# A 64-row tile with high and low halves in one stationary operand, and attention tails by Newton steps on GpSimd

## The reference, cut to what matters

```python
h = rmsnorm(x, norm_x)                      # x: 1024 prompt rows, 64 sample rows, 1024 wide
aq, ak, av, az, gq, gk, gv, gz, gr, mq, mz, gl = split(h @ w_in)
aq, ak = rmsnorm(aq per 64, g_qa), rmsnorm(ak per 64, g_ka)
p = softmax(aq @ ak.T / 8 + alibi, causal)  # two maps a head; samples also attend to paged keys
oa = (p[0] - lam * p[1]) @ av
oa = rmsnorm(oa per 128, g_oa) * (1 - lam_init)
ua = (oa * silu(az)) @ w_branch[0]
ub = (rmsnorm(gla(gq, gk, gv, gr), g_ob) * silu(gz)) @ w_branch[1]
um = (softmax(rmsnorm(mq per 128, g_qm) @ mem_k.T) @ mem_v * silu(mz)) @ w_branch[2]
y = x + (sigmoid(g_a) * ua + sigmoid(g_b) * ub + sigmoid(g_m) * um) @ w_o
```

## Time and profile before

| | |
|---|---|
| Median of three runs | 1357.0 us (1356.37 to 1358.52) |
| The profiled execution | 1358.5 us, of which the span 1356.7 us |
| PE | busy 1292.0 us, 95% of the span, 7846 matmuls |
| DVE | 546.9 us, 40% |
| ACT | 477.3 us, 35% |
| GpSimd | 108.5 us, 8% |
| PE's clock | nine tenths of full speed or more in 37 of the page's 40 slices, eight tenths in three |

### The profile page before, as it was taken

The page is one execution under the profiler, slowest core; times in us unless marked ns, Lnnn a source line. Parts: engine busy times, 40 slices in busy tenths (PEclk is TensorE's granted clock), DMA queues, the critical chain, the costliest instruction groups (busy, mean ns, idle before and its releaser), DMA issues.

```text
span 1356.7 us, 19404 instructions
## 1 busy us (share of the span) xinstructions
PE 1292.0 (95%) x7846; PEld 1115.6 (82%) x7846; DVE 546.9 (40%) x1187; ACT 477.3 (35%) x1064; POOL 108.5 (8%) x126
## 2 busy tenths in 40 slices
PE   6999999999877899999899999999999999999998
PEld 5778788888756786788777887788999999999876
DVE  5654344566673325277743443312222222222411
ACT  5543223655665225256632433212221111212200
POOL 0010000000001000000111000000122221222000
PEclk9999999999998899999899999999999999999999
DMA  8432111110004331101212303431011131110422
GB/s 273 145 101 82 47 39 44 32 32 20 13 0 153 92 114 33 32 24 45 80 49 69 103 24 105 129 113 47 24 47 48 47 109 47 47 48 17 155 86 70
DMA packets 89930, 94.47 MB, mean 70 GB/s; under 512 B 8498, under 2 KB 64626, under 8 KB 89714
## 3 DMA queue, kind: packets, MB, share of 16 engines
q1 hardware_dynamic: 85506, 79.33, 19.3%
q0 software_dynamic: 4336, 13.90, 2.8%
HBM read 79.32 MB, written 13.89 MB: 69 GB/s over the span
## 4 chain that ended last, share of the span: by engine, by line
PE 87%; ACT 5%; DVE 4%; issue 2%; DMA 1%; SPq 0%; POOLq 0%; POOL 0%; ACTq 0%; DVEq 0%
PE heavy L835 14%; PE heavy L837 14%; PE heavy L836 14%; PE heavy L847 9%; PE heavy L849 8%; PE heavy L848 8%; PE heavy L897 4%; PE scores L947 2%; PE attended L967 1%; PE transposed L956 1%; PE scores L1208 1%; PE transposed L924 1%; PE scores L1107 1%; PE attended L1226 1%; ACT arena L1496 1%
## 5 line engine op out<-in xcount | busy, mean ns | idle before, releaser
L1369 ACT ACTIVATE arena<-heavy 128x364 f32<-128x364 f32 (+1 forms) x108 | 50.9, 471 | 366.4 <-PE heavy L837 366.3
L835 PE MATMUL heavy<-h_hi,rc_hi 128*128 128x364 f32 (+1 forms) x384 | 131.9, 343 | 0.0
L836 PE MATMUL heavy<-h_lo,rc_hi 128*128 128x364 f32 (+1 forms) x384 | 127.4, 332 | 0.0
L837 PE MATMUL heavy<-h_hi,rc_lo 128*128 128x364 f32 (+1 forms) x384 | 127.4, 332 | 0.0
L835 PE MATMUL heavy<-h_hi,rp_hi 128*128 128x364 f32 (+1 forms) x384 | 126.3, 329 | 0.0
L836 PE MATMUL heavy<-h_lo,rp_hi 128*128 128x364 f32 (+1 forms) x384 | 126.1, 328 | 0.0
L837 PE MATMUL heavy<-h_hi,rp_lo 128*128 128x364 f32 (+1 forms) x384 | 126.1, 328 | 0.0
L1824 DVE SCALAR_TENSOR_TENSOR arena<-arena,heavy 128x364 f32<-128x364 f32 (+1 forms) x48 | 25.5, 532 | 211.4 <-PE heavy L837 211.4
L614 POOL TENSOR_TENSOR merged<-merged,arena 128x364 f32<-128x364 f32 (+1 forms) x48 | 66.8, 1392 | 441.7 <-DVE arena L1824 441.7
L835 PEld LDWEIGHTS heavy<-h_hi,rc_hi 128*128 128x128 f32 x384 | 73.7, 192 | 4.0 <-issue 3.1
L836 PEld LDWEIGHTS heavy<-h_lo,rc_hi 128*128 128x128 f32 x384 | 73.6, 192 | 0.0
(11 more groups left out here) (312 smaller groups left out, 2896.5 us busy)
## 6 DMA issues: line engine op xcount, KB each, us to landing
out<-arena POOLq DMA_DIRECT2D x36, 256.0 KB, 3.3
rc_whole<-w_in SPq DMA_DIRECT2D x16, 512.0 KB, 3.9
rp_whole<-w_in SPq DMA_DIRECT2D x16, 512.0 KB, 4.0
arena<-x_prompt SPq DMA_DIRECT2D x8, 512.0 KB, 5.7
arena<-cache_k_a SPq DMA_DIRECT2D x16, 256.0 KB, 3.2
arena<-cache_v_a SPq DMA_DIRECT2D x16, 256.0 KB, 3.5
ra_whole<-w_in SPq DMA_DIRECT2D x8, 512.0 KB, 4.1
arena<-cache_mem_k SPq DMA_DIRECT2D x8, 512.0 KB, 4.6
```

Of the source, the lines that this page charges most:

```text
L835: nc.tensor.matmul(out, a_hi, b_hi, start=(x == 0), stop=False)
L836: nc.tensor.matmul(out, a_hi, b_lo, start=False, stop=False)
L837: end = nc.tensor.matmul(out, a_lo, b_hi, start=False, stop=(x == len(terms) - 1))
L1369: nc.scalar.activation(tanh[m % 2][:, 0:cw], bank[:, 0:cw], ACT.Tanh, scale=0.5)\
```

## The change

Two things are changed. **The sample tile's products.** `h_hi` is widened by 64 columns, so that for the sample tile the high half and the low half stand side by side as one stationary operand of 128 (`sample_product`). Two matmuls a slice, by the weights' high and low half, make 16 instead of 24; rows 0 to 63 of the bank then hold the products of the high half, rows 64 to 127 those of the low half. ACT copies the lower 64 rows to SBUF, DVE adds them onto the upper ones, and from there on the work is as before. DVE makes the low half a second time, into the widened columns. In V the sample tile now stands before tile 7, in Q behind tile 0, and in the second half of O before tile 7.

**The tails of the prompt.** ACT takes the squares only; no other table is loaded. One unit later DVE adds the epsilon term and makes a first guess of the reciprocal root by integer arithmetic (`tail_guess`); GpSimd improves it by three Newton steps of four instructions on 128x4 elements, each waiting for the one before (`tail_newton`); DVE scales without a reciprocal. The tails of the other branches and of the samples are as before.

For room, one table (`comb`, 64 KB) is moved into the shared arena, and its transfer stands behind the first value pages in SP's queue; PE's first `sample_weights` waits for it. The core of the diff:

```diff
-    add("V", [("rows", "gv", r) for r in range(PT + 1)])
+    add("V", [("rows", "gv", r) for r in (*range(PT - 1), PT, PT - 1)])
     add("MZ", cols("mz", KW))
-    add("Q", [("rows", "mq", r) for r in range(PT + 1)])
+    add("Q", [("rows", "mq", r) for r in (0, PT, *range(1, PT))])
     add("PA", pairs(0))
     add("PB", pairs(1))
     add("PM", pairs(2))
-    add("O", [("out", r, j) for j in range(2) for r in range(PT + 1)])
+    add("O", [("out", r, 0) for r in range(PT + 1)] + [("out", r, 1) for r in (*range(PT - 1), PT, PT - 1)])
...
-        h_hi, h_lo, h_whole = trio("h", 0, 8704, [KD, T])
+        h_hi = part("h_hi", -TAIL, [KD, T + NS_TOK])
+        h_lo, h_whole = part("h_lo", 8704, [KD, T]), part("h_whole", 8704, [KD, T], F32)
...
+            def settle(ins):
+                steps[0] += 1
+                ins.then_inc(newton, 1)
+                pool.wait_ge(newton, steps[0])
+            def tail_newton(k):
+                x, y, a = ostat[:, 0, :], ostat[:, 2, :], ohalf[:, :]
+                pool.wait_ge(guessed, k + 1)
+                for i in range(3):
+                    settle(pool.tensor_tensor(out=a, in0=y, in1=y, op=ALU.mult))
+                    settle(pool.tensor_tensor(out=a, in0=a, in1=x, op=ALU.mult))
+                    settle(pool.tensor_scalar(a, a, -0.5, 1.5, ALU.mult, ALU.add))
+                    end = pool.tensor_tensor(out=y, in0=y, in1=a, op=ALU.mult)
+                    if i < 2:
+                        settle(end)
+                end.then_inc(oroot_done, 1)
+            for k in range(PT - 1):
+                tail_newton(k)
...
+            tail_newton(PT - 1)
...
+            sp.wait_ge(pv_done, NU)
+            sp.dma_start(comb, tab["comb"]).then_inc(comb_in, 16)
...
+            def sample_product(n, kind, bank):
+                w_hi, w_lo, _ = W4[kind]
+                for k in range(KD):
+                    both = h_hi[:, k, NP_TOK:T + NS_TOK]
+                    nc.tensor.matmul(bank[:, :], both, w_hi[:, k, :], start=(k == 0), stop=False)
+                    end = nc.tensor.matmul(bank[:, :], both, w_lo[:, k, :], start=False, stop=(k == KD - 1))
+                end.then_inc(hv_full[n % 2], 1)
...
+                    if t == PT:
+                        sample_product(n, kind, bank)
+                        return
...
+                if b == 0:
+                    pe.wait_ge(comb_in, 16)
...
+                    if sample_rows(n):
+                        nc.scalar.copy(low_rows_of(n), bank[NS_TOK:P, :]).then_inc(low_rows, 1)
+                        act.wait_ge(rows_added, sample_rows(n))
...
-                    settle(nc.scalar.activation(waste[:, :], og[:, h * P:(h + 1) * P], ACT.Square,
-                                                accum_out=ostat[:, 0, h:h + 1]))
-                for h in range(H):
-                    end = nc.scalar.activation(ostat[:, 1, h:h + 1], ostat[:, 0, h:h + 1], ACT.Sqrt,
-                                               bias=ssq[:, h:h + 1], scale=1.0 / P)
-                end.then_inc(oroot_done, 1)
+                    end = nc.scalar.activation(waste[:, :], og[:, h * P:(h + 1) * P], ACT.Square,
+                                               accum_out=ostat[:, 0, h:h + 1])
+                    if h < H - 1:
+                        settle(end)
+                end.then_inc(squares_done, 1)
+                act.wait_ge(squares_done, k + 1)
...
+                if sample_rows(n):
+                    dve.wait_ge(low_rows, sample_rows(n))
+                    nc.vector.tensor_tensor(out=bank[0:NS_TOK, :], in0=bank[0:NS_TOK, :], in1=low_rows_of(n), op=ALU.add)\
+                        .then_inc(rows_added, 1)
...
+                if t == PT:
+                    hi, _, whole = tile_of(t)
+                    low((hi, sample_low, whole))
...
+            def tail_guess(k):
+                x, y = ostat[:, 0, :], ostat[:, 2, :]
+                dve.wait_ge(squares_done, k + 1)
+                settle(nc.vector.scalar_tensor_tensor(out=x, in0=x, scalar=1.0 / P, in1=ssq[:, :], op0=ALU.mult, op1=ALU.add))
+                settle(nc.vector.tensor_scalar(y.bitcast(I32), x.bitcast(I32), 1, None, ALU.logical_shift_right))
+                nc.vector.tensor_scalar(y.bitcast(I32), y.bitcast(I32), -1, 0x5F3759DF, ALU.mult, ALU.add).then_inc(guessed, 1)
             def tail_scale(k):
                 n = tail_rows(k)
                 dve.wait_ge(oroot_done, k + 1)
-                settle(nc.vector.reciprocal(ostat[0:n, 2, :], ostat[0:n, 1, :]))
+                if k >= PT:
+                    settle(nc.vector.reciprocal(ostat[0:n, 2, :], ostat[0:n, 1, :]))
...
+                if u - 1 in A_END:
+                    tail_guess(A_END[u - 1])
...
+            tail_guess(PT - 1)
             tail_scale(PT - 1)
```

More of the change, by code:

```diff
@@ L87, in shape_tables @@
     return {k: np.ascontiguousarray(v, dtype=np.float32) for k, v in tabs.items()}
-SMALL = ["ident", "batch", "slope", "isl", "map", "comb", "gmask"]
+SMALL = ["ident", "batch", "slope", "isl", "map", "gmask"]
 def heavy_jobs():
@@ L264, in hybrid_step @@
         arena_base = -(-nc.sbuf_base // 32) * 32
-        arena = sb("arena", [P, 51928])
+        TAIL = 512
+        arena = sb("arena", [P, TAIL + 51928])
         def shaped(v, shape):
@@ L311, in hybrid_step @@
         vpage = [at(41472 + 1024 * i, [NPG, W]) for i in range(2)]
+        comb = at(44544, [P])
         past_t, new_t = at(43520, [PAST]), at(43776, [NB, NS_TOK])
@@ L370, in hybrid_step @@
         gx, gmem = sb("gx", [P, KD]), sb("gmem", [P, KD])
-        gka_row, gkm_row = sb("gka_row", [P, 64]), sb("gkm_row", [P, P])
+        gka_row, gkm_row = at(51712, [64]), at(21504, [P])
         ba_col = sb("ba_col", [P, 2])
@@ L376, in hybrid_step @@
         rstat = sb("rstat", [P, 3])
-        ostat = sb("ostat", [P, 3, H])
+        ostat, ohalf = sb("ostat", [P, 3, H]), sb("ohalf", [P, H])
         ssum, ssq, waste = sb("ssum", [P, 2, H]), sb("ssq", [P, H]), sb("waste", [P, P])
@@ L413, in hybrid_step @@
         qpad_zero, qpad_ready, new_keys = sem("qpad_zero"), sem("qpad_ready"), sem("new_keys")
-        tabs_in, pt_in = sem("tabs_in"), sem("pt_in")
+        tabs_in, comb_in, pt_in = sem("tabs_in"), sem("comb_in"), sem("pt_in")
         k_in, v_in = [sem("k_in0"), sem("k_in1")], [sem("v_in0"), sem("v_in1")]
@@ L418, in hybrid_step @@
         o_full, o_free, oroot_done = sem("o_full"), sem("o_free"), sem("oroot_done")
+        guessed, squares_done, newton = sem("guessed"), sem("squares_done"), sem("newton")
         ob_free = sem("ob_free")
@@ L436, in hybrid_step @@
         lam_exp = sem("lam_exp")
+        low_rows, rows_added = sem("low_rows"), sem("rows_added")
         def map_of(u, c):
@@ L445, in hv_wait_free, with sample_rows, low_rows_of @@
             eng.wait_ge(hv_free[n % 2], n // 2 + 1)
+        def sample_rows(n):
+            j = JOBS[n]
+            if (j[0], j[1]) == ("out", PT) or (j[0] == "rows" and j[2] == PT):
+                return sum(1 for x in JOBS[:n + 1] if (x[0], x[1]) == ("out", PT) or (x[0] == "rows" and x[2] == PT))
+            return 0
+        sample_low = h_hi[:, :, T:T + NS_TOK]
+        def low_rows_of(n):
+            kind = "out" if JOBS[n][0] == "out" else JOBS[n][1]
+            return {"gv": at(TL, [W]), "mq": sq_m, "out": at(44544, [W])}.get(kind, sq)[0:NS_TOK, :]
         def bc(ap, k):
@@ L557, in _ @@
                         pool.dma_start(mk_kept, mk_first).then_inc(mk_out, 16)
+            steps = [0]
+            def settle(ins):
[15 more added lines that the diff above has]
+                tail_newton(k)
             pool.wait_ge(sc_read, 2 * NU)
@@ L869, in heavy @@
                         pe.wait_ge(mt_split, r + 1)
+                    if r == PT:
+                        sample_product(n, f"o{x}", bank)
+                        return
                     a_hi, a_lo = m_first if r == 0 else (h_hi[:, :, c], h_lo[:, :, c])
@@ L1033, in sample_weights @@
                     end = nc.tensor.matmul(TR[0:m, j * P:(j + 1) * P], Ps[b % 2][:, j * P:j * P + m],
-                                           small["comb"][:, :], start=True, stop=True)
+                                           comb, start=True, stop=True)
                 end.then_inc(tr_full, 1)
@@ L1748, in _ @@
                     set_high("o1", r - 3)
+            for j in range(2):
+                n = job("out", PT, j)
+                hv_wait_full(act, n)
+                act.wait_ge(rows_added, sample_rows(n) - 1)
+                nc.scalar.copy(low_rows_of(n), HV[n % 2][NS_TOK:P, :]).then_inc(low_rows, 1)
         @block.vector
@@ L1828, in heavy @@
                     x = n - STAGE["O"][0]
+                    if sample_rows(n):
+                        dve.wait_ge(rows_added, sample_rows(n))
                     hv_wait_full(dve, n)
@@ L1889, in _ @@
                         constants()
+                    if r == PT:
+                        heavy(n)
                     x_evict(r + 2)
```

(6 more changed lines are left out.)

9 lines of the change are left out of this document (5 added, 4 removed).

## The result

The changed kernel takes 1340.6 us (median of four of its five executions, 1334.23 to 1341.72) against 1357.76 before; the ratio is 0.9864 (95% interval 0.9836 to 0.9893). The forecast was 1340.0 within 1332 to 1350. The profiled execution took 1334.2 us with a span of 1332.5, so it is the shortest of the five, not the middle one; the four others took 1339.8 to 1341.7.

What follows compares the result with a forecast made beforehand. TensorE (PE), with 87% of the chain of waits, was taken as the bound. Products with the end (-9.4 us) and tails (-7.5) summed to -16.9, from a median of 1357.0 to 1340 us, range 1332 to 1350.

Steps and rivals of the forecast that it cites:

- rival 6: Sample products: with 128 stationary columns the pitch grows to 0.34, so 16 matmuls cost as 24; 1349.5 us, chance 0.02.
- seven products: Sample tile's v, q, k, gv, mq and two output products: 16 matmuls for 24, 1.82 us each where PE is the limit.
- The moved table: Ring table ahead of the gv weights in SP's queue, its transfer waiting until the last attention product: 0 us.
- The end: Last output transfer, 256 KB rather than 128 KB: the end 0 to 1.65 us later, taken as +0.8.
- Tail 6: Sixth attention tail, an unfilled step: PE's step shrinks by ACT's removed 3.4 us, plus 1.0 of lower clock: -4.4.
- Tail 5: Fifth attention tail: PE's waits of 1.11 for the eviction and 0.81 for DVE behind it go: -1.9 us.
- tail 7: Seventh attention tail: PE's idle time falls by 1.75 us, less 0.6 for DVE's guess instructions: -1.2.
- tails 1 to 4: First four attention tails, in steps filled with PE's own columns: 0 us, to -1.
- Rival 3: Tails: GpSimd and DVE get in each other's way, two unfilled tails give back 3 us each: 1346, chance 0.06.
- The slow rival: Tails: GpSimd's Newton steps, at 1.25 us each, overrun their room and DVE and PE wait: 1363 us, chance 0.03.
- The clock: PE's stretches at the lower clock, behind idle places: two more or fewer give 1343.5 or 1336.5 us; as a rival, chance 0.06.
- signs of being wrong: Copy and add in PE's waits, lower clock where it was not, or the end over 1.7 us later behind PE's last matmul.

Runs made afterwards that it cites:

- products_only: The changed kernel with the prompt's tails as before (ACT's roots and table loads, no Newton steps), sample products kept: 1350.1 us, ratio 0.9941 to the kernel before.
- tails_only: The changed kernel with the sample products as before (24 matmuls, old order of jobs), Newton tails kept: 1348.8 us, ratio 0.9933 to the kernel before.
- newton_dve: The changed kernel with the Newton steps on DVE, right behind the guess, instead of on GpSimd: 1348.7 us, ratio 0.9936 to the kernel before.
- newton_long: The changed kernel with 12 Newton steps instead of 3, so 48 GpSimd instructions a tail: 1366.8 us, ratio 1.0055 to the kernel before.
- after_again: The changed kernel run once more with no edit, for its spread: 1341.7 us, ratio 0.9877 to the kernel before.
- old_order: The changed kernel with the sample tile last again in V, Q and both halves of the output: 1347.6 us, ratio 0.9921 to the kernel before.

## Why the prediction was right, and where not

The steps in the prediction's order, by the first profile where nothing else is said:

- **The pitch and the seven products.** The pitch of 0.23 held, so rival 6 fell. v -0.9 (forecast -1.0), q -1.9 (-1.8), k -0.5 (-0.5), gv -1.9 (-1.8), mq -1.6 (-1.5), outputs -3.8 (-3.6). The moved table: nothing, as forecast; PE's wait ahead of the first sample weights is 3.74 before and 3.75 after.
- **The end.** Forecast +0.8, measured 0: from PE's last start to the end 7.1 us before and after, although the last transfer has grown from 128 to 256 KB. My term took half of the landing time as growing with the size. The packets of the last transfer show that it does not here: they move for 0.76 us before (1352.17 to 1352.94) and 0.83 after (1327.90 to 1328.73), and in both traces 3.7 to 3.8 us follow them to the end of the span. The products sum to -10.6 instead of -9.4.
- **Tails.** Tail 6: the step shrank by 3.5 (forecast 3.4), and the lower clock behind it is absent in both profiles: -0.9 (forecast -1.0, by setting 2.91 against the 1.78 of smaller scores; the same scores take 1.99). Tail 5 -2.2 (-1.9), tail 7 -2.0 (-1.2: the two waits gave 2.7, the guess took 0.7 of it), tails 1 to 4 -1.1 (0, bound -1), tail 8 nothing. The wait for the first key page shrank by 0.6 (3.65 to 3.02), which no term had. It is as short in products_only (3.11) and in tails_only (3.07), so it belongs to neither part alone, and its cause stays open. Sum -8.8 without the clock and -9.4 with the 0.6, where the forecast had -6.5; tails_only measured -9.1.
- **GpSimd.** 12 x 0.28 = 3.4 us against 3.5, from the copies' pitch: right, up to 4.5 where a step is held up. Rival 3 fell: DVE's times are unchanged (751 ns for the 128x512 combination before and after). GpSimd is the one held up, its longest Newton instruction taking 1.06 us against a median of 0.20: in the first profile each of the ten that took over 0.3 us started beside a DVE instruction with two SBUF inputs and ended 0.05 to 0.06 us behind it. The Trainium skill's rule on the shared port pair ("SBUF — State Buffer", "SBUF: two separate sides") agrees with that in kind. DVE waited for GpSimd at the last tail alone, where it had waited for ACT before, so the hold-ups cost PE nothing that the traces show. The Trainium skill's other rule, that elementwise work belongs on VectorE ("GPSIMD Engine Reference", "Engine selection"), names the shorter chain here too, though by a factor of 1.4 (2.5 us on DVE against 3.4) and not by two; yet that kernel, newton_dve, is the slower one. By queue, not by speed, the choice was right.
- **The slow rival's price.** I gave the first six tails 14 us of room, from the table load to DVE's question. From GpSimd's start it is 9.7 to 13.4. For the seventh the text has near 11 and the formula 8; it is 5.4. My formula gives 13.7 us for newton_long's 13.5 us chain (s = 1.13) and still a gain; measured were 25 and a loss. At the eighth tail it is right (8.1 and 8.1); at the fifth and sixth it has nothing where PE lost 4.7 and 3.9. The rooms were too large, and the slower clock behind each new wait was left out.
- **The clock.** I took it as a side case of 3.5 us either way, and the sum with one stretch less. By PE's markers the parts are worth 20.0 us (10.6 and 9.4) without the clock, where the terms without it sum to 15.9. The median gained 17.2, so some 3 us went to more time at the lower clock, behind the k joint, the first key page and the V joint, where I had 1 us of gain. So that the predicted median met the measured one within 1 us is luck: two errors of opposite sign, the parts some 4 us too small, and the clock too good by about as much. One of the prediction's own signs of being wrong did come up: in after_again the lower clock appears at the V joint (573.7 to 580.5), where the trace of the kernel before has none. Where the clock falls is shown by the two profiles of one kernel; for the executions that were only timed it is argued from their mean clocks.

## What to carry to other kernels

A product with a narrow stationary operand pays by moving columns, so two narrow operands side by side cost as one. Their added copy and add are free where a further full product stands behind (1.3 us at each of three joints in old_order, where none does); put the narrow tile next to last. A serial chain of tiny instructions belongs on the engine with the empty queue, not the fast one, and its bound is the room between its start and its reader. Fill PE's idle places first by order: each costs its wait and, in some executions, as much or more again in slower PE time behind it (in after_again 3.0 us at the first key page, then 10 us at half speed: PEclk 0.80 over 25).

## What was not expected of the hardware

The spread of one and the same kernel, 1334.2 to 1344.3 us, goes with the mean granted clock: 1334.2 at 0.991, 1339.4 to 1339.9 at 0.984, 1341.3 to 1341.7 at 0.983, 1344.1 and 1344.3 at 0.981, with PE's waits at the three places the same to 0.1 us in the two profiles compared. The lower level mostly followed places where PE had stood idle for 1.6 to 4 us, not each time; once, at 734.1 in after_again, only two waits of 0.7 and 0.8 stood ahead of it. A GpSimd instruction on 128x4 elements, 0.20 us by the median, took up to 1.06 beside DVE's two-input instructions, while DVE's times did not move. And an output transfer of twice the size did not move the end of the span by more than 0.1 us.
